# Differential attention: the low parts of four weight units move from GpSimd to VectorE, in quarters

## The reference, cut to what matters

```python
def diff_attention(q, k, v, lam):          # 8 heads, q blocks of 128 queries
    ...
        sc = jnp.einsum('bqhtd,bkhtd->bhtqk', q_i, kf) * scale
        p = jax.nn.softmax(jnp.where(mask, sc, neg), axis=-1)
        w = p[:, :, 0] - lam * p[:, :, 1]
        return jnp.einsum('bhqk,bkhe->bqhe', w, vf)
...
o = rmsnorm(o, sub_norm_b[j]) * (1.0 - lambda_init)
y = (o * jax.nn.silu(gate)) @ w_out_b[j]
```

## Time and profile before

| | |
|---|---|
| median of 3 runs | 2152.12 us (2151.99 to 2152.35) |
| profiled execution | 2154.83 us, of which 2152.8 us are the span of the trace |
| PE busy | 2047.5 us, 95% of the span |
| DVE busy | 817.5 us, 38% |
| ACT busy | 737.5 us, 34% |
| POOL busy | 781.2 us, 36% |
| mean granted clock of PE | 0.979 of full speed |

### The profile page before, as it was taken

One profiled execution on the slowest core, in us unless ns is written; L12 is line 12 of the kernel. 1 busy time (PEld: TensorE's weight loads), 2 busy tenths in 40 slices (PEclk: granted clock), 3 DMA queues, 4 the chain that ended last, 5 costly groups with the idle time before them and its releaser, 6 DMA issues.

```text
span 2152.8 us, 31449 instructions
## 1 busy us (share of the span) xinstructions
PE 2047.5 (95%) x13672; PEld 1750.0 (81%) x13672; DVE 817.5 (38%) x1280; ACT 737.5 (34%) x1089; POOL 781.2 (36%) x248
## 2 busy tenths in 40 slices
PE   7999999989988888999999989999999999999998
PEld 5898888868866677999999877799777788888886
DVE  3400675135347646220122251257466554211222
ACT  5333223335546534221222244342222233222222
POOL 3443332545412135434443332024334234434332
PEclk9999999999999998999999999999999999999999
DMA  5223122222310121323322431022113132223312
GB/s 169 87 91 113 50 73 79 91 75 79 98 59 20 40 69 49 99 67 101 107 73 74 112 89 58 30 76 79 41 56 114 60 98 82 90 88 113 98 62 76
DMA packets 170033, 171.48 MB, mean 80 GB/s; under 512 B 16924, under 2 KB 160664, under 8 KB 169896
## 3 DMA queue, kind: packets, MB, share of 16 engines
q1 hardware_dynamic: 168492, 167.25, 24.5%
q10 hardware_dynamic: 1404, 2.23, 0.3%
HBM read 163.17 MB, written 6.29 MB: 79 GB/s over the span
## 4 chain that ended last, share of the span: by engine, by line
PE 88%; DVE 4%; issue 3%; ACT 2%; POOL 1%; DMA 1%; ACTq 0%; SPq 0%; DVEq 0%; POOLq 0%
PE ps L2059 86%; PE ps L2061 2%; POOL w_lo L748 1%; ACT w_hi L885 0%; ACT diag L913 0%; DMA x_rows<-in_x 0%; DVE gdn_x L1924 0%; DVE coef L1561 0%; POOL stat L765 0%; DVE gdn_inv_t L1907 0%; DVE mla_q L1727 0%; DVE sg L1549 0%; ACT u_hi L939 0%; DMA ret_decay<-c_decay 0%; DVE diff_norm L1574 0%
## 5 line engine op out<-in xcount | busy, mean ns | idle before, releaser
L748 POOL TENSOR_TENSOR w_lo<-w_raw,w_hi 128x2048 fp32r<-128x2048 f32 (+3 forms) x157 | 674.2, 4297 | 951.0 <-ACT w_hi L885 945.5
L2059 PE MATMUL ps<-u_hi,w_hi 128*128 128x512 f32 (+1 forms) x1904 | 594.5, 352 | 38.1 <-DVE sg L1549 12.3
L2059 PE MATMUL ps<-u_lo,w_hi 128*128 128x512 f32 (+1 forms) x1904 | 584.7, 347 | 0.0
L2059 PE MATMUL ps<-u_hi,w_lo 128*128 128x512 f32 (+1 forms) x1904 | 584.3, 347 | 0.0
L2059 PEld LDWEIGHTS ps<-u_hi,w_hi 128*128 128x128 f32 x1904 | 332.8, 191 | 86.1 <-issue 31.1
L2059 PEld LDWEIGHTS ps<-u_hi,w_lo 128*128 128x128 f32 x1904 | 331.8, 191 | 41.4 <-issue 0.5
L2059 PEld LDWEIGHTS ps<-u_lo,w_hi 128*128 128x128 f32 x1904 | 332.5, 191 | 38.3 <-issue 0.9
L885 ACT ACTIVATE w_hi<-w_raw 128x2048 fp32r<-128x2048 f32 (+3 forms) x157 | 279.6, 1783 | 178.4 <-PE ps L2059 169.0
L2059 PE MATMUL ps<-hidden_hi,w_hi 128*128 128x264 f32 (+1 forms) x528 | 141.1, 321 | 0.0
L2059 PE MATMUL ps<-hidden_lo,w_hi 128*128 128x264 f32 (+1 forms) x528 | 141.0, 322 | 0.0
L2059 PE MATMUL ps<-hidden_hi,w_lo 128*128 128x264 f32 (+1 forms) x528 | 140.8, 321 | 0.0
(11 more groups left out here) (370 smaller groups left out, 2892.6 us busy)
## 6 DMA issues: line engine op xcount, KB each, us to landing
w_raw<-in_w_in_a SPq DMA_DIRECT2D x23, 1024.0 KB, 5.2
w_raw<-in_ffn_w_gate SPq DMA_DIRECT2D x22, 1024.0 KB, 5.3
w_raw<-in_ffn_w_up SPq DMA_DIRECT2D x22, 1024.0 KB, 5.3
w_raw<-in_w_in SPq DMA_DIRECT2D x17, 1024.0 KB, 5.3
w_raw<-in_ffn_w_down SPq DMA_DIRECT2D x16, 768.0 KB, 4.3
w_raw<-in_ffn_w_down SPq DMA_DIRECT2D x16, 640.0 KB, 4.0
w_raw<-in_w_out_a SPq DMA_DIRECT2D x8, 1024.0 KB, 5.0
w_raw<-in_w_kv SPq DMA_DIRECT2D x8, 1024.0 KB, 5.3
```

Source lines behind the costliest of these rows:

```text
L748: pool.tensor_tensor(WL[:, u % RAWS, part], RAW[:, u % RAWS, part], WH[:, u % SPLITS, part].bitcast(F32), ALU.subtract).then_inc(lo_done, 1)
L2059: return nc.tensor.matmul(o, a, b, start=start, stop=stop, **kw)
```

## The change

The four whole-unit subtractions are taken out of POOL's loop. DVE does them instead, each as four quarters of 128x512, one quarter behind diff_w in steps a + 1 to a + 4 for a = 0, 9, 17 and 25. Each quarter waits for the unit's high part; the last one waits also for the low part of the unit before, and counts lo_done. POOL waits before its next subtraction until DVE has finished the last of the four units.

```diff
@@ POOL
             for s in range(ITEMS + HEAD_LAG):
-                if s in (0, 9, 17, 25):
-                    lo(j_diff_gate.unit0 + s // 8 + 2)
                 if s >= 8 and (s - 8) % NT == 0 and (s - 8) // NT < HEADS:
...
+            pool.wait_ge(lo_done, j_diff_out.unit0 + 3)
             split(j_diff_out)
@@ DVE
             dve.wait_ge(lam_step, 5)
+            lo_steps = {a + 1 + q: (j_diff_gate.unit0 + i + 2, q) for i, a in enumerate((0, 9, 17, 25)) for q in range(4)}
             for s in range(ITEMS + HEAD_LAG):
...
                     nc.vector.scalar_tensor_tensor(out=DW[:, g % 2, 0:n], in0=DE[:, g % 2, 1, 0:n], scalar=COEF[:, 0:1],
                                                    in1=DE[:, g % 2, 0, 0:n], op0=ALU.mult, op1=ALU.add).then_inc(da_w, 1)
+                if s in lo_steps:
+                    u, q = lo_steps[s]
+                    part = slice(q * UNIT // 4, (q + 1) * UNIT // 4)
+                    dve.wait_ge(hi_done, u + 2)
+                    if q == 3:
+                        dve.wait_ge(lo_done, u + 1)
+                    last = nc.vector.tensor_tensor(WL[:, u % RAWS, part], RAW[:, u % RAWS, part],
+                                                   WH[:, u % SPLITS, part].bitcast(F32), ALU.subtract)
+                    if q == 3:
+                        last.then_inc(lo_done, 1)
                 if s >= 7 and (s - 7) % NT == 0 and (s - 7) // NT < HEADS:
```

## The result

| | before | after |
|---|---|---|
| median of 21 runs each, on the same chips | 2151.30 us | 2155.69 us |
| lowest to highest | 2149.05 to 2156.09 | 2151.16 to 2162.06 |
| profiled execution (span) | 2154.83 (2152.8) | 2161.71 (2159.7) |
| mean granted clock in it | 0.979 | 0.975 |

The ratio is 1.0023, with a 95% interval of 1.0017 to 1.0029: the changed kernel is 4 to 5 us slower, where 0.1 us was forecast. Its runs also lie further apart.

The account below looks back on a forecast made before the run. PE, holding 88% of the chain, bounds the kernel; DVE and POOL count only through PE's idle. Adding +0.14 us to the profiled 2154.83 gives 2154.97, less 2.71 to the median: 2152.3 us, range 2150.2 to 2154.9.

Parts of the forecast that it names:

- The lock: Attention stage: POOL's four subtractions block DVE, costing it 14.5 us; PE feels 1.74 us, which removing them gives back.
- PE's three chains: Steps 11, 19, 27, from mask matmuls through DVE's sg to PE's return: made late by 0.49, 0.75, 0.50 us.
- The quarters: Sixteen DVE subtractions of 0.684 us, 0.61 in the queue; those of steps 11, 19, 27 exposed, the others essentially in gaps.
- that of step 3: Quarter with 0.58 us of gap before the reduce of step 4: 0.03 us sticks out, put down as 0.05.
- The waits on w_hi: DVE in quarter 0: ACT finishes w_hi 0.7 us before DVE would arrive; a late one has 3 us of gap.
- its upper bound of 0.79 us: Queue time of one quarter if its wait instructions prevent overlap and cost 0.1 us; PE's sum would be +0.84 us.
- The sum for PE: PE's idle in steps 12, 20, 28: +0.12, -0.14, +0.11 us; step 4: +0.05; together +0.14 us.
- the 2.0 that was named: Sign of being right: PE idle near 2.3, 2.0, 2.3 us after steps 11, 19, 27; this is the second.
- the rival on PE's clock: Attention-stage idles gain or lose one or two half-clock episodes, 1.7 to 3.4 us; fewer 0.12, more (or lock not lifted) 0.15.
- another count of half-clock stretches after 660 us: Sign of being wrong: PE runs at half clock in more or fewer stretches after 660 us than before; no size given.
- could reach +5 us: More half-clock episodes, each of the stage's head changes losing 1.7 us; chance 0.05, shared with exposed quarters.
- another rival: Quarters exposed in all sixteen attention steps, gaps not covering them: +8.1 us, 2160 us; chance 0.05, shared with three more episodes.

Follow-up runs that it names:

- the kernel without low parts: Kernel before, POOL subtracting only 8 columns of each of the four units, PE multiplying the high part again instead of the low part: 2151.89 us, 1.0003.
- The version with hidden quarters: Changed kernel with the exposed quarters moved one step on, so none stands in the chain before sg in steps 3, 11, 19, 27: 2151.03 us, 0.9999.

## Why the prediction was wrong

*The lock.* Right. DVE's four swollen operations are gone. In the kernel without low parts 14.7 us of DVE's time came back, and PE's three chains are 0.48, 0.75 and 0.48 us shorter, 1.71 us in all (1.74 by the sum); at equal clock its gain is 2.0 us. The lock is as the Trainium skill states it ("SBUF — State Buffer", section "SBUF: two separate sides"); how much of it the kernel feels is decided by the chain.

*The quarters.* Right: 0.684 us each, 0.60 in the queue, three exposed, the others in gaps, that of step 3 too. The waits on w_hi never held DVE up. The prediction counted two wait instructions per quarter and three in the last; the diff has one and two, which only its upper bound of 0.79 us used.

*The sum for PE.* +0.12, -0.14 and +0.11 us were forecast and +0.13, -0.14 and +0.12 measured. Only the idle before PE's return in step 20 is 2.30 us and not the 2.0 that was named. The return came as forecast, but before the change DVE's late diff_w also held PE's transposes back by 0.27 us (they started at 693.39, and start at 693.12 now, with the mask matmuls of the step at 691.97 in both), which had cut the idle that followed. An idle time alone is not the length of the chain.

*The step that failed* is the rival on PE's clock: that "three idles changed by 0.1 us each can gain or lose one or two such episodes", weighed at 0.15 on the slow side and "nearly all within 0.2%". One of the prediction's own signs of being wrong, another count of half-clock stretches after 660 us, is what came. Two things were wrong in it. It looked for lost clock only at the three head changes of the attention stage. In the profiles the clock fell at other places inside the stage without a net loss (0.93 in both), and the loss lies behind the stage, in the output projection and the latent attention, whose idles the change does not alter but whose start it moves; the delayed versions of before show that a delay alone is enough, and the one at 1290 us shows it for the latent attention by itself. A delay just behind the attention stage left it undecided (1.0006). And it took the kernel before as a middle, from which a new draw goes either way. Before is a low point of its own column, so nearly every disturbance loses: 0.0009 to 0.0030 for the four delays before the stage. In the profiled execution the change did not add one or two stretches that cost 1.7 us each but 18 us of half clock, 9 us of lost pace. The prediction did say that the clock "could reach +5 us", with a chance of 0.05 shared with another rival. The size is near what came, but it was to come from the stage's head changes, so this is luck and not a forecast.

*The range* (2150.2 to 2154.9) had one episode more on the slow side; 2155.69 us is 0.8 us above it. It held the change's own cost and not the cost of moving; the six delayed versions of before, with medians from 2153.65 to 2158.71, are the range that it ought to have had above.

*What stays open.* Why this alignment of before is a good one, and which stretch decides in an undisturbed run, is not settled: each build has one profiled execution, and both of the changed kernel happened to be near its upper end (2161.7 and 2161.9 us). The clock is also drawn anew from execution to execution of one program: the two profiled ones of before took 2154.8 and 2149.4 us, at a clock of 0.979 and 0.982. A net 0.14 us of delay in front of the stage costs half of what the change costs (1.0009 against 1.0017 to 1.0023, intervals that overlap); the rest may come from PE's changed times inside the stage or from the draw. A version with PE's clock held fixed was not tried. The version with hidden quarters beats the changed kernel and ties with the kernel before; in the means over the delays and at equal clock it is the best of the three, but its 1.9 us are smaller than what the alignment gives or takes.

## What to carry to other kernels

Before you believe a difference of some tenths of a per cent in a kernel where PE stands still at many places, time the old kernel with a few harmless delays of 0.1 to 2 us: their scatter is the real uncertainty of the comparison, even when the runs of one build agree to 0.1%. A kernel that was picked for its time may well sit at the low end of it, as the kernel before does here. Compare two versions by their means over the same delays, or at equal granted clock. And price an operation by the chain in which it stands: sixteen equal quarters cost nothing in thirteen places and 0.6 us in three.

## What the runs showed of the hardware

A delay of about 0.14 us on DVE at 609 us moved the median by 2.7 us (2154.23 against 2151.57 on the same chip; ratio 1.0009, interval 1.0001 to 1.0018), and one of 1.2 us moved it by 7.2 us (2158.71 against 2151.51), while 1.9 us moved it by 3.7. One idle of PE of 1.49 us was followed by 3.5 us at the lower clock level in one execution and by 13.6 us in another, with the same instructions behind it.

Under POOL's subtraction of 4.53 us, VectorE's operations on two SBUF inputs stood until it ended, even one of a single column (coef, 128x1, 4.12 us in place of 0.22), while a reduce from PSUM and the reciprocal ran at their usual 0.69 and 0.15 us (615.97 and 616.58, under the first subtraction).
